# Moving the residual add of the last stage from VectorE to GpSimd

## The reference, cut to what matters

```python
def second_block(x, ..., final_norm_w):
    x = x + mixer(h, w_in[l], ...)
    h = rmsnorm(x, norm2_w[l])
    x = x + hier_moe(h, ..., w_gate[l], w_up[l], w_down[l])
    return rmsnorm(x, final_norm_w)
```

## Time and profile before

| what | value |
|---|---|
| time, median of three runs | 2623.24 us |
| span of the profiled execution, first to last instruction | 2627.9 us |
| VectorE busy, whole span | 765.4 us (29%) |
| GpSimd busy, whole span | 573.0 us (22%) |
| first load of the last stage issued at | 2588.84 us |
| VectorE in the last stage, first instruction to end of the last | 2593.70 to 2624.84 us |

### The profile page before, as it was taken

One profiled execution on the slowest core, in us unless ns is written; L12 is line 12 of the kernel. 1 busy time (PEld: TensorE's weight loads), 2 busy tenths in 40 slices (PEclk: granted clock), 3 DMA queues, 4 the chain that ended last, 5 costly groups with the idle time before them and its releaser, 6 DMA issues.

```text
span 2627.9 us, 42507 instructions
## 1 busy us (share of the span) xinstructions
PE 2365.7 (90%) x18656; PEld 1541.1 (59%) x18656; DVE 765.4 (29%) x1615; ACT 549.4 (21%) x1147; POOL 573.0 (22%) x409
## 2 busy tenths in 40 slices
PE   8999998788799999999999998999999889888983
PEld 7887776677676654788787455443334344443441
DVE  4111325565445523323223343211111111111115
ACT  4111223342455412211111121110111011010102
POOL 5343333231111113413322001111111111111110
PEclk9999999999899999999999998999999999999997
DMA  4223110102110021211112406999999999999996
GB/s 192 93 99 123 67 67 27 35 3 90 58 65 1 1 88 65 84 37 57 56 45 77 200 32 259 418 429 430 429 429 429 429 429 429 430 428 430 429 429 260
DMA packets 69649, 537.41 MB, mean 205 GB/s; under 512 B 12920, under 2 KB 13176, under 8 KB 43472
## 3 DMA queue, kind: packets, MB, share of 16 engines
q1 hardware_dynamic: 55200, 505.99, 46.6%
q0 software_dynamic: 10240, 16.82, 1.7%
q10 hardware_dynamic: 4016, 11.80, 1.4%
HBM read 503.08 MB, written 43.52 MB: 208 GB/s over the span
## 4 chain that ended last, share of the span: by engine, by line
PE 70%; DMA 18%; DVE 6%; ACT 4%; issue 3%; POOL 0%; POOLq 0%; SPq 0%; DVEq 0%; ACTq 0%
PE banks L219 45%; DMA arena<-in_wg 16%; PE banks L224 8%; PE banks L226 8%; PE banks L225 8%; DMA arena<-in_con 1%; ACT arena L229 1%; ACT arena L1602 1%; PE banks L2829 1%; DVE arena L1581 0%; DVE arena L2805 0%; DVE arena L1127 0%; DVE arena L3095 0%; DVE arena L3102 0%; DVE arena L3100 0%
## 5 line engine op out<-in xcount | busy, mean ns | idle before, releaser
L219 PE MATMUL banks<-arena 64*64 64x64 f32 (+14 forms) x15424 | 1692.4, 350 | 198.4 <-DMA arena<-in_wg 59.9
L219 PEld LDWEIGHTS banks<-arena 64*64 64x64 f32 (+5 forms) x15424 | 983.6, 157 | 847.8 <-issue 691.7
L229 ACT ACTIVATE arena<-banks 128x512 f32<-128x512 f32 (+6 forms) x381 | 219.7, 587 | 1431.2 <-PE banks L219 627.9
L2823 POOL DMA_INDIRECT yb<-arena x64 | 64.9, 1015 | 805.7 <-DVE arena L2937 805.7
L2937 DVE TENSOR_SCALAR arena<-banks,arena 128x512 f32<-128x512 f32 x64 | 48.0, 751 | 511.7 <-PE banks L219 511.7
L224 PE MATMUL banks<-h1h,w2s 128*128 128x512 f32 x448 | 177.0, 395 | 1.7 <-DVE h1l L1967 1.7
L225 PE MATMUL banks<-h1l,w2s 128*128 128x512 f32 x448 | 175.0, 391 | 0.0
L226 PE MATMUL banks<-h1h,w2s 128*128 128x512 f32 x448 | 174.8, 390 | 0.0
L224 PE MATMUL banks<-hh,wlo 128*128 128x512 f32 x432 | 172.8, 400 | 0.0
L226 PE MATMUL banks<-hh,wlo 128*128 128x512 f32 x432 | 171.1, 396 | 0.0
L225 PE MATMUL banks<-hl,wlo 128*128 128x512 f32 x432 | 170.0, 394 | 0.0
(11 more groups left out here) (242 smaller groups left out, 1522.4 us busy)
## 6 DMA issues: line engine op xcount, KB each, us to landing
arena<-in_wg SPq DMA_DIRECT2D x64, 2048.0 KB, 33.0
arena<-in_wu SPq DMA_DIRECT2D x64, 2048.0 KB, 26.7
arena<-in_wd SPq DMA_DIRECT2D x64, 2048.0 KB, 31.2
arena<-in_w SPq DMA_DIRECT2D x55, 512.0 KB, 3.3
spill<-arena SPq DMA_DIRECT2D x27, 512.0 KB, 2.6
arena<-spill SPq DMA_DIRECT2D x27, 512.0 KB, 4.6
arena<-in_wo SPq DMA_DIRECT2D x16, 512.0 KB, 7.2
arena<-yb SPq DMA_DIRECT2D x8, 1024.0 KB, 12.1
```

The source lines that it names most:

```text
L219: return pe.e.matmul(o, l, r, start=start, stop=stop)
L229: return act.e.activation(o, i, ACT.Copy)
L2823: return pool.e.indirect_dma_start(yb, bass.IndirectOffsetOnAxis(ap=six[:, col:col + 1].bitcast(U32), axis=0), src[:, :], None, bounds_che ...
```

## The change

GpSimd gets a part in the last stage: for each block it adds the residual to the second expert's rows, in place, as soon as the block's load has landed. VectorE waits for that and adds the two halves. The number of adds is the same (16 of 128 x 1024), eight of them are now on GpSimd.

```diff
         for j in range(8):
             y = yl[j][:, 0:D]
             dve.wait_ge(s(f"x{j}"), 48)
-            dve.e.tensor_tensor(y, y, yl[j][:, D:2 * D], ALU.add).then_inc(s("y_sum").sem, 1)
             dve.wait_ge(s("y_sum"), j + 1)
-            dve.e.tensor_tensor(y, y, xres[:, j, :], ALU.add).then_inc(s("y_res").sem, 1)
+            dve.e.tensor_tensor(y, y, yl[j][:, D:2 * D], ALU.add).then_inc(s("y_res").sem, 1)
             if j:
                 scale(j - 1)
         scale(7)
+
+    def pool_final(pool):
+
+        for j in range(8):
+            second = yl[j][:, D:2 * D]
+            pool.wait_ge(s(f"x{j}"), 48)
+            pool.e.tensor_tensor(second, second, xres[:, j, :], ALU.add).then_inc(s("y_sum").sem, 1)
```

More of the change, by code:

```diff
@@ L3183, in _ @@
         over(pool, pool_over)
+        pool_final(pool)
     @block.sync
```

## The result

The changed kernel takes 2630.95 us (median of 20 runs, 2626.25 to 2635.12), the kernel before 2625.11 us (median of 20 runs, 2619.78 to 2628.56). The ratio is 1.0026 with a 95% interval of 1.0019 to 1.0032: slower by 0.26%, which is 6.8 us (5.0 to 8.4). The ratio is estimated from all the runs and is not the quotient of the two medians, which lie 5.8 us apart; both are inside the interval.

What follows compares the result with a forecast made beforehand. VectorE bounds the last 31 us: eight adds gone (-10.1), eight GpSimd adds in its way (+18.1), hidden start-ups (-0.8), a 0.42 us wait gone. Step by step +6.6, so 2623.24 + 6.6 = 2629.8 us (+0.25%), range 2624.5 to 2633.5.

Steps and rivals of the forecast that it cites:

- What bounds the kernel: Last stage: VectorE bounds the last 31 us; an add less per block worth up to 10 us if GpSimd is free.
- side by side: Rival, last stage: GpSimd's adds run hidden beside VectorE's work, stage 5.1 us shorter, 2618.1 us; chance 0.06.
- P: GpSimd's residual add per block in the last stage: 2.35 us alone, 2.25 us behind a waiting turn.
- The two engines take turns: Last stage: VectorE instructions with two SBUF inputs and such GpSimd ones don't overlap; only about 0.14 us start-up is hidden.
- A: VectorE's add of the two halves per block, last stage: 1.22 us alone, 1.08 us behind a GpSimd add.
- T: VectorE's scaling instruction per block, last stage, reading rows and gain: 1.28 us alone, 1.14 us behind a GpSimd add.
- The order of turns: Last stage: after two GpSimd adds in a row the engines alternate without gap, then VectorE goes on alone, 2.53 us per pair.
- The sum: Last stage: step-by-step end of VectorE's last scaling moves from 2624.84 to 2631.47 us, 6.6 us longer.
- A sign that did not come: Last stage: the chain of waits must run through GpSimd from 2593.7 to about 2618.6 us.
- The rule set beside the rows: Skill page's some 115 ns hand-over, added for 13 turns in the last stage: 1.5 us more, 8.1 instead of 6.6.
- Cheap P: Rival, last stage: GpSimd's add costs only 1.95 us alone, 1.79 behind a turn; +3.0 us, 2626.2 us; chance 0.12.
- Dearer turns: Rival, last stage: turns or GpSimd's adds cost 0.1 to 0.3 us more each; +7.5 to +9 us, 2631 to 2632; chance 0.10.

Runs made afterwards that it cites:

- e1: Changed kernel with GpSimd's adds taken out and the residual left out of the output; 2621.66 us, ratio 0.9987 to the kernel before.
- e4: Changed kernel with GpSimd adding the halves and VectorE reading residual and gain from PSUM, copied by ScalarE; 2621.51 us, ratio 0.9986 to the kernel before.
- e3: Changed kernel with the gain copied once to PSUM by ScalarE and read there by VectorE's scaling; 2626.4 us, ratio 1.0002 to the kernel before.
- e7: Changed kernel with GpSimd adding the two halves and VectorE adding the residual from PSUM; last stage 29.37 us, against 37.39 in the changed kernel.
- e8: Changed kernel with GpSimd's add replaced by a copy of the residual over the second expert's rows; last stage 27.67 us, against 37.39.
- e5: Changed kernel with GpSimd's add replaced by a multiplication by 1.0, residual left out; last stage 30.28 us, against 37.39.

## Why the prediction was right

By its own steps:

- *What bounds the kernel.* VectorE, and no longer once its work falls. That held for this change. But the prediction said that an add less on each block could be worth up to 10 us if GpSimd's work is free, and that the last store finds free transfers; of the 39.1 us between first load and end, e1 gained only 4.7 and e4 4.4. That step would have failed had the change worked: my price for the rival "side by side", 5.1 us, is about what e4 gives (4.4 us in the profile, 3.7 in the time), but with P taken away altogether (e1) the stage's 7.8 us became 4.7.
- *The two engines take turns.* Read from another stage, and seen here in each turn from P1 to T2; e3, e7 and e4 show that it hangs on VectorE's second input from SBUF, and they remove the wait without removing work.
- *Price of P.* 2.34 us alone (2.35 said) and 2.20 behind a turn (2.25 said). *Price of A and T behind a P*: 1.08 both (1.08 and 1.14 said).
- *The order of turns* was P1 P2 A1 P3 T0 P4 A2 P5 T1 P6 A3 P7 T2, as written down. The end of T2 was 25.65 us after the start, 26.02 predicted; the lone pairs behind it took 2.53 us each, as predicted.
- *The sum.* + 6.6 us predicted, + 6.25 in the stage and + 6.8 us (5.0 to 8.4) in the time. What is missing in the stage is six or so P at 0.05 less and three T at 0.06 less, against a hand-over of 0.10 us instead of 0.04 before A0. That 6.6 and 6.8 lie so close is partly luck: the interval is 3.4 us wide, and the medians give 5.8. The pieces that the prediction then names in words add up to 6.8 and not 6.6, since they leave out that three hand-overs of 0.04 us are hidden under a P as well; the forecast used the step-by-step sum.
- *A sign that did not come.* The prediction wanted the chain of waits to run through GpSimd up to P7's end. It goes through P1 alone (3.00 us), because that view cannot show a wait for a turn; the durations and ends, which were the other signs, did show it.
- *The rule set beside the rows*, some 115 ns on top of each turn, would have given + 8.1 us. The Trainium skill, page "SBUF — State Buffer", section "A bandwidth-pool intuition that's wrong (but worth ruling out)", gives that figure for a transfer issued by GpSimd that waits for a copy on VectorE; to carry it over to two computing instructions was the prediction's step, and it is not borne out: every lag behind the other engine's turn in the stage (1.08 and 2.20 us) is at or under that of the earlier trace rows. The same page says in its section "Who interferes with whom" that an instruction of VectorE with two SBUF inputs contends with a GpSimd instruction that reads SBUF, and that one with at most one, outside the modes in which VectorE uses two ports, doesn't. The traces of e3, e4 and e8 agree (T 1.28 us beside P with one such input, 3.17 with two). Its section "SBUF: two separate sides" says that the one that starts first has the ports for its whole instruction and the other is blocked. For the adds here the trace agrees; for e5 it does not, where the wait was 0.90 us of 2.64, and the measurement decides.
- *The rivals.* Side by side: not in this kernel; it is e4. Cheap P: no, P took 2.34 us alone. Dearer turns: no, no turn behind the other engine's was above its price; P2, directly behind P1, took 2.29 us for 2.25. This rival's + 7.5 to + 9 us is the price for eight turns; thirteen at 0.1 to 0.3 us would have been + 7.9 to + 10.5.

## What to carry to other kernels

Before work is moved from VectorE to GpSimd, count the inputs from SBUF of what stays on VectorE: if they are two, a GpSimd instruction that reads SBUF takes turns with VectorE's, and the move pays only when the time for which it holds VectorE up is shorter than that of the instruction that it takes off. Here that was 2.20 us for an add against 1.26, which lost; a copy would have cost 0.90. VectorE's large instructions with a single input, and GpSimd instructions that only write, were not tried. Look for a pair of such instructions anywhere in the trace. The sign is one whose duration is too long by the rest of the other engine's instruction, since no view of waits shows it. One of the two inputs in PSUM, copied there by an idle ScalarE, parts the engines (0.26% slower became 0.14% faster here), and the next bound, here the transfers, should be looked up before more is hoped for.

## What the runs showed of the hardware that was not expected

A multiplication by a constant on GpSimd (128 x 1024, one input) ran 2.79 us alone and kept a two-input instruction of VectorE waiting for 0.90 us only, while an add of two inputs kept it waiting for its whole 2.20 us. For the same shape with one input a copy ran 1.04 us and the multiplication 2.79.
